# Two-layer encoder trunk, latent attention: the exponential one slot later, VectorE's masked maximum ahead of the low halves, and the rotary tables built under layer 0's down projection

## What is computed

```python
# rotary tables, needed by layer 1 alone
freqs = 500000 ** (-arange(half) / half)
cos, sin = cos(positions * freqs), sin(positions * freqs)

# layer 0
x = layer_norm(ALPHA * x + mixer_sb_fox(x, ...), ...)
x = layer_norm(ALPHA * x + (gelu(conv(x @ w_gate)) * (x @ w_up)) @ w_down, ...)

# layer 1: 16 query heads over one shared latent key of 256 numbers
logits = einsum('bqhd,bqkd->bqhk', q, k_sel) * scale      # k_sel: each query's best 256 keys
p = softmax(where(valid, logits, -inf))
ctx = einsum('bqhk,bqkc->bqhc', p, k_sel[..., 64:])
```

## Time and profile before

| | us |
|---|---|
| median of three runs | 3183.16 |
| the profiled execution | 3195.31 |
| its span in the profile | 3193.5 |
| TensorE busy / weight loads | 2943.2 / 1524.1 |
| VectorE busy | 1805.8 |
| GpSimd busy | 1442.3 |
| ScalarE busy | 1026.3 |
| mean granted TensorE clock | 0.975 |

### The profile page before, as it was taken

One profiled execution on the slowest core, in us unless ns is written; L12 is line 12 of the kernel. 1 busy time (PEld: TensorE's weight loads), 2 busy tenths in 40 slices (PEclk: granted clock), 3 DMA queues, 4 the chain that ended last, 5 costly groups with the idle time before them and its releaser, 6 DMA issues.

```text
span 3193.5 us, 45888 instructions
## 1 busy us (share of the span) xinstructions
PE 2943.2 (92%) x17190; PEld 1524.1 (48%) x17472; DVE 1805.8 (57%) x2540; ACT 1026.3 (32%) x1671; POOL 1442.3 (45%) x721
## 2 busy tenths in 40 slices
PE   5899997999999999959799999888889999999998
PEld 3556665444444444434344444555654444444443
DVE  7687556474444414154699999566655744444042
ACT  3556667112222200014653334445540221222000
POOL 3577221654344378644017776200006533443785
PEclk8999999999999999979899999999999999999999
DMA  4222321411111132211003222011103111111322
GB/s 145 65 57 63 74 57 27 165 54 53 53 52 46 53 106 93 86 60 53 13 6 126 105 105 90 32 51 39 39 26 120 53 53 53 52 46 53 112 99 99
DMA packets 96516, 218.24 MB, mean 68 GB/s; under 512 B 41328, under 2 KB 41456, under 8 KB 96416
## 3 DMA queue, kind: packets, MB, share of 16 engines
q1 hardware_dynamic: 54048, 195.74, 18.0%
q10 hardware_dynamic: 42368, 21.11, 2.8%
HBM read 176.92 MB, written 23.12 MB: 63 GB/s over the span
## 4 chain that ended last, share of the span: by engine, by line
PE 39%; DVE 8%; ACT 5%; issue 3%; POOL 1%; DVEq 0%; DMA 0%; ACTq 0%; POOLq 0%; SPq 0%
PE ps L301 24%; PE ps L312 8%; PE ps L1865 3%; DVE prob L1942 2%; DVE score L1588 1%; DVE pt_lo L1934 1%; PE ps L336 1%; ACT strip_w L1534 1%; ACT strip_w L1449 1%; ACT pt_hi L1913 1%; PE ps L1901 1%; PE ps L1681 1%; ACT prob L1923 1%; PE ps L1880 1%; POOL w_hi L271 0%
## 5 line engine op out<-in xcount | busy, mean ns | idle before, releaser
L271 POOL TENSOR_TENSOR w_hi<-w_stage,ones 128x1024 bf16<-128x1024 f32 x227 | 454.8, 2004 | 940.2 <-PE ps L301 540.3
L301 PE MATMUL ps<-xt_hi,w_hi 128*128 128x512 bf16 x1888 | 565.4, 380 | 33.9 <-ACT strip_f L1450 29.7
L301 PE MATMUL ps<-xt_lo,w_hi 128*128 128x512 bf16 x1889 | 566.0, 380 | 1.6
L301 PE MATMUL ps<-xt_hi,w_lo 128*128 128x512 bf16 x1880 | 563.6, 380 | 2.1
L274 POOL TENSOR_TENSOR w_lo<-w_stage,w_hi 128x1024 bf16<-128x1024 f32 x227 | 520.4, 2292 | 17.8
L301 PEld LDWEIGHTS ps<-xt_hi,w_hi 128*128 128x128 bf16 x1920 | 187.9, 98 | 259.6 <-issue 29.8
L301 PEld LDWEIGHTS ps<-xt_hi,w_lo 128*128 128x128 bf16 x1920 | 188.3, 98 | 227.7 <-issue 2.1
L301 PEld LDWEIGHTS ps<-xt_lo,w_hi 128*128 128x128 bf16 x1920 | 188.2, 98 | 227.4 <-issue 1.6
L1219 DVE SCALAR_TENSOR_TENSOR x_res<-x_res,ps 128x1024 f32<-128x1024 f32 x32 | 38.9, 1216 | 417.8 <-PE ps L312 417.8
L1347 DVE TENSOR_SCALAR conv_up<-gate_up,conv_w_up 128x1024 f32<-128x1024 f32 x44 | 78.4, 1782 | 283.2 <-ACT gate_up L1328 282.7
L312 PE MATMUL ps<-w_hi,hid_hi 128*128 128x512 bf16 x689 | 206.2, 379 | 5.6 <-DVE x_res L1219 4.0
(11 more groups left out here) (230 smaller groups left out, 5746.2 us busy)
## 6 DMA issues: line engine op xcount, KB each, us to landing
w_stage<-in_l_up SPq DMA_DIRECT2D x88, 512.0 KB, 3.3
w_stage<-in_l_down SPq DMA_DIRECT2D x88, 512.0 KB, 3.3
w_stage<-in_l_o SPq DMA_DIRECT2D x32, 512.0 KB, 3.9
w_stage<-in_l_q SPq DMA_DIRECT2D x32, 512.0 KB, 5.4
q_split<-q_out SPq DMA_DIRECT2D x32, 512.0 KB, 2.6
q_now<-q_split SPq DMA_DIRECT2D x16, 1024.0 KB, 4.9
w_stage<-in_l_qkv SPq DMA_DIRECT2D x24, 512.0 KB, 3.5
k_twice<-nk_hi ACTq DMA_DIRECT2D x32, 128.0 KB, 2.9
```

The costliest lines, as they stand in the source:

```text
L271: pool.tensor_tensor(w_hi[slot][:, 0:cols], w_stage[slot][:, 0:cols], ones[:, 0:1].to_broadcast([P, cols]), ALU.mult).then_inc(w_cast[slot ...
L301: mm = pe.matmul(ps[:, bank + h, :], w, a[:, k, h * HALF:(h + 1) * HALF], start=(first and k == k0 and m == 0), stop=(last and k == k1 - 1 ...
```

## The change

Three edits. (1) All rotary work (two loads, 22 VectorE instructions, 4 sines, 4 stores) moves from the opening and the heads stage to the down projection of layer 0, in front of its `accumulate(0)` on VectorE and its square roots on ScalarE; its buffers move onto `xt_hi`/`xt_lo`. In the opening ScalarE now copies the four query and key halves, issues the 12 query and key copies, and only then takes the two value halves. (2) In latent attention ScalarE takes the exponential of the slot before, not of its own slot. (3) VectorE takes maximum(s) and `neg_max`(s) before `pt_lo`(s-3).

```diff
@@ start_sync
-            sp.dma_start(pos_i[:, :], t_in["positions"]).then_inc(s_pos, 16)
-            sp.dma_start(rope_rows[:, :], t_in["rope_rows"]).then_inc(s_pos, 16)
@@ start_vector
-            rotary_angles(dve, 0)
@@
-        scratch = Room(room.at)
+        scratch = Room(xt_at)
+        rope_rows = scratch("rope_rows", [P, 4], F32)
@@ pair_scalar
-                    if prev is None and at == 0:
-                        act.wait_ge(s_tabst, 64)
@@ heads_scalar
-            rotary_sines(act, 0)
-            rotary_store(act, 0)
-            proj_evac_hi(act, 0, 0)
-            proj_evac_hi(act, 1, 0)
-            rotary_sines(act, 1)
             act.preload_act_table_set("sigmoid_and_others")
-            for e in range(2, 6):
+            for e in range(4):
                 proj_evac_hi(act, e, 0)
             for hh in range(2):
                 make_current_qk(act, hh, 0)
+            for e in range(4, 6):
+                proj_evac_hi(act, e, 0)
             for hh in range(2):
                 make_current_v(act, hh, 0)
-            rotary_store(act, 1)
@@ heads_vector
-            rotary_finish(dve, 0)
-            proj_evac_lo(dve, 0, 0)
-            proj_evac_lo(dve, 1, 0)
-            rotary_angles(dve, 1)
-            proj_evac_lo(dve, 2, 0)
-            proj_evac_lo(dve, 3, 0)
-            rotary_finish(dve, 1)
-            proj_evac_lo(dve, 4, 0)
-            proj_evac_lo(dve, 5, 0)
+            for e in range(6):
+                proj_evac_lo(dve, e, 0)
@@ new
+        def rotary_sync(sp):
+            sp.dma_start(pos_i[:, :], t_in["positions"]).then_inc(s_pos, 16)
+            sp.dma_start(rope_rows[:, :], t_in["rope_rows"]).then_inc(s_pos, 16)
+
+        def rotary_scalar(act):
+            for t in range(2):
+                rotary_sines(act, t)
+                rotary_store(act, t)
+            act.wait_ge(s_tabst, 64)
+
+        def rotary_vector(dve):
+            for t in range(2):
+                rotary_angles(dve, t)
+                rotary_finish(dve, t)
@@ back_and_norm, sync_program (dn0 alone)
                 if after:
                     sp.wait_ge(after["hidden_lo"], FT)
+                if rotary:
+                    rotary_sync(sp)
                 sp.dma_start(g_rows[:, :], names[0]).then_inc(s_gb, 16)
@@ latent_scalar
-                if kind:
-                    t, i, hh = slot, query_block(slot), slot // 8
+                p, t = steps_behind(act, pair, slot, kind, prev, 1)
+                if t is not None:
+                    i, hh = query_block(t), t // 8
                     n = span[i]
-                    act.wait_ge(t_nm, STEPS * pair + t + 1)
+                    act.wait_ge(t_nm, STEPS * p + t + 1)
@@ latent_vector: this block moves from before the maximum to after neg_max
                 p, t = steps_behind(dve, pair, slot, kind, prev, SUMS_LAG + 1)
                 if t is not None:
                     for n, j0, m in batch_list(t):
                         hi, lo, src = turned_views(t, n, j0, m)
                         dve.wait_ge(t_hi, BATCHES * p + n + 1)
                         dve.tensor_tensor(lo, src, hi, ALU.subtract).then_inc(t_lo, 1)
```

More of the change, by code:

```diff
@@ L200, in program @@
         w_lo = [wroom(f"w_lo{s}", [P, KT * P], BF16) for s in range(SLOTS)]
+        xt_at = wroom.at
         xt_hi = wroom("xt_hi", [P, KT, SEQ], BF16)
@@ L375, in program @@
         xt_f = room("xt_f", [P, KT, SEQ], F32)
-        rope_rows = room("rope_rows", [P, 4], F32)
         wf_f = room("wf_f", [P, KT, 8], F32)
@@ L969, in heads_sync @@
             load_first(sp, feed_o0)
-            sp.wait_ge(s_tabst, 64)
         def heads_gpsimd(pool):
@@ L1041, in back_and_norm @@
         def back_and_norm(tag, feed, tiles, act_hi, act_lo, names, free_at, bank_of, next_feed, early, load_x=None,
-                          final=None, after=None, started=None):
+                          final=None, after=None, started=None, rotary=False):
             room = Room(free_at)
@@ L1097, in sync_program @@
                     load_first(sp, next_feed)
+                if rotary:
+                    sp.wait_ge(s_tabst, 64)
                 if final is not None:
@@ L1194, in highs @@
                         act.activation(hi, src, ACT.Copy).then_inc(s_nh, 1)
+                if rotary:
+                    rotary_scalar(act)
                 for i in range(GROUP):
@@ L1246, in lows @@
                         dve.tensor_tensor(lo, src, hi, ALU.subtract).then_inc(s_nl, 1)
+                if rotary:
+                    rotary_vector(dve)
                 for i in range(GROUP):
@@ L1396, in program @@
             back_and_norm("dn0", feed_down0, FT, hid_hi, hid_lo, (t_in["l0_ln2_g"], t_in["l0_ln2_b"]),
-                          after_hid, (0, 4, 2, 6), feed_small, early_small(feed_small), after=up0_sems))
+                          after_hid, (0, 4, 2, 6), feed_small, early_small(feed_small), after=up0_sems, rotary=True))
         clear_sems()
@@ L1928, in latent_vector @@
             for slot in lat_slots(kind):
[L1929 to L1934, removed]
                 if kind:
@@ L1947, in latent_vector @@
                                       None, ALU.mult).then_inc(t_nm, 1)
+                p, t = steps_behind(dve, pair, slot, kind, prev, SUMS_LAG + 1)
+                if t is not None:
+                    for n, j0, m in batch_list(t):
+                        hi, lo, src = turned_views(t, n, j0, m)
+                        dve.wait_ge(t_hi, BATCHES * p + n + 1)
+                        dve.tensor_tensor(lo, src, hi, ALU.subtract).then_inc(t_lo, 1)
                 p, t = steps_behind(dve, pair, slot, kind, prev, SCALE_LAG)
```

## The result

Median of five runs 3198.9 us, against 3184.2 us for the kernel before on the same chip: ratio 1.0048, 95% interval 1.0034 to 1.0063, +14.7 us. The forecast was 3197 us, +13.5. The profiled executions don't show this difference: both spans are 3193.5 us. The changed kernel's is its fastest execution (3195.3 against a median of 3198.9), the one of before lies 11 us over its median of 3184.2.

The account below looks back on a forecast made before the run. TensorE, busy 2943 of 3193.5 us, was taken as the bound, so only its stands count. Opening -25.5, down projection 0, latent stage +37, clock +2 sum to +13.5 on 3183.2: 3197 us, range 3179 to 3226.

Parts of the forecast that it names:

- the main term: Latent stage: maximum ahead of `pt_lo` closes a new circle in which TensorE stands; +37 us, bounds 28 to 44.
- Opening: Opening: without rotary work ScalarE's first sigmoid comes earlier and TensorE stands less; -25.5 us, gain bounds 21 to 28.
- Down projection: Layer 0's down projection: added rotary work fits VectorE's 104.8 idle us, GpSimd stays ahead; 0 us, bounds 0 to +4.
- the exclusive lock: Down projection: skill's claim that VectorE and GpSimd fully block each other; by it the cost would be nearer +4.
- Latent stage at full clock: Latent halves grow from 24.15 to 26.74 and 26.29 us as TensorE waits for `pt_lo`; +37 us, bounds 28 to 44.
- Clock in the latent stage: Latent stage: TensorE's clock mostly stays up; +2 us, bounds 0 to 46 (16 halves x 2.9).
- rival C: Latent stage: clock falls in most halves, 12 x 2.9 = 35 us on top of 37, total 3230; chance 0.18.
- Rival A: Latent stage: freed ScalarE shortens the slots, at most 71 us; 3122 with half of it; chance 0.10.

Follow-up runs that it names:

- e1: Only the rotary move, latent stage as before, against the kernel before: 3167.2 us, ratio 0.9940.
- e5: Rotary move and exponential a slot later, VectorE's latent order kept, against the kernel before: 3093.3 us, ratio 0.9713.
- e6: As e5, but GpSimd's first weight piece waits for VectorE's last `xt_lo`: 3095.7 us against e5's 3093.3.
- e7: The kernel before, unchanged, profiled once more: span 3185.1 us against 3193.5 in its first profile.
- e2: Only the two latent edits (exponential a slot later, maximum ahead of low halves), no rotary move, against the kernel before: 3222.1 us, ratio 1.0111.
- e4: Only VectorE's maximum ahead of the low halves, exponential in its own slot, against the kernel before: 3220.8 us, ratio 1.0107.
- e9: As e2, but only the second batch of low halves of a slot goes behind the maximum, against the kernel before: 3147.0 us, ratio 0.9874.
- e3: Only the exponential a slot later, VectorE's low halves still ahead of the maximum, against the kernel before: 3116.3 us, ratio 0.978.

## Why the prediction was right, term by term

The forecast named the right mechanism for the main term and its place. That the total came within 1.2 us (+13.5 against +14.7) is luck: single terms were off by 6 to 9 us, with both signs.

**Opening, -25.5 predicted, -19 measured** (e1; first `stay` -20.2). What was mis-sized is one term: "Leaving the two loads out of SyncE's queue brings the first weight piece about 1.3 us earlier, but then GpSimd lies beside more of VectorE's `xt_lo`; between -1 and +1, I take 0". The piece was split from 13.45 on, not from 16.52, and lay beside all five `xt_lo`: 13.02 us instead of 7.65, projections from 27.18, ended at 58.57 instead of 53.8. That is +5 on the path of the value copies (+3 in e5). The term was named and mis-sized; its bounds would have had to be as wide as the slowing (3.04 against 1.21) over five instructions allows, 9 us. The gain, 20.2 at the first `stay`, lies outside the forecast's bounds of 21 to 28. The lower one stood for gate sums fully beside GpSimd, but 26.1 + 12.4 + 16 is 54.5, more than 9 us beyond the 45 of the same text. That the gate sums ended within the forecast 42 to 45 (43.4) is luck: their scan began at 31.75, some 5 us late, and they were hardly slowed. Full clock from 60 on (to 82) held; whether it gave back the 1.4 us no run separates, since e1's interval is 15 to 24 us.

**Down projection, 0 predicted, 0.0 measured** (104.79 against 104.78). GpSimd's first ten pieces took 4.5 to 5.9 us, 5.1 on average where the forecast had "near 5.9", and TensorE stood for none (busy 9.95 of every 10 us from 1104 to 1174). Against the exclusive lock (the Trainium skill, SBUF — State Buffer, Who interferes with whom) the forecast held that "both engines are slowed and neither stops". The rows don't show that: a row gives an instruction's start and length, not whether the engine stood within it.
```profile
1139.89 8.93 DVE L939 SCALAR_TENSOR_TENSOR angle<-turns,angle 128x1024 f32<-128x1024 f32 x3
1141.81 2.87 POOL L272 TENSOR_TENSOR w_hi<-w_stage,ones 128x1024 bf16<-128x1024 f32 x1
1144.75 2.99 POOL L275 TENSOR_TENSOR w_lo<-w_stage,w_hi 128x1024 bf16<-128x1024 f32 x1
```
In the 5.9 us of this piece VectorE does two of its three. Alone, the piece takes 4.0 us, and two such instructions 2.4 (the two `xt_lo` of e6), 6.4 together: close to taking turns, as by the lock. It would have each VectorE instruction cost GpSimd its whole 1.2 us; the piece grew by 1.9 for two. So the lock is neither refuted nor in full agreement here, and GpSimd kept ahead of TensorE, at 5.1 us a piece against 5.19.

**Latent stage at full clock, +37 predicted, about +28 measured.** The mechanism and its place were right, slot by slot: 4.19, 4.63, 3.91, 3.32 and 2.76 against 4.29, 4.72, 4.02, 3.41 and 2.85. Each is 0.1 too long in the forecast, mostly for one reason: `pt_lo` starts 0.99 us after the maximum (2030.92 to 2031.91), where the sum had 1.01 and a gap of 0.05, and the maximum starts 0.30 and not 0.31 after the last scores. Times five slots and 16 halves that is 8 us. The stage's tail, from the last slot's scores to the last values, was also 2.8 us shorter (6.7 against 9.5), and 1.4 of these are the clock: it fell in the tail of the first profile of before, and in e7, where it didn't, the tail is 8.1. The value lies at the lower bound of 28 to 44 (37 less and plus the 8 of the forecast would be 29 to 45).

**Clock in the latent stage, +2 predicted, +10.5 measured in the profile, 9 more than before.** The clock fell in eight halves of 16, each time at about the start of slot 4, and cost 0.8 to 1.6 us a time, not 2.9. Where it fell at the start, slot 4 took 5.22 us instead of 3.91, the 1.3 us that its own scores take longer at half clock; slot 5, which the forecast had slow too, kept its 3.32 to 3.35 in every half. So the frequency lies between the forecast ("a few halves") and rival C (12), and a fall cost about half or less of what both took. Rival C also misread: slot 3's 2.6 us of work in 4.7 is no share "between the two rows" but a larger one than either (2.62 and 2.40 of 5), and the clock fell all the same. The Trainium skill's TensorE: Matmul & The Clock Gate, HAM oscillation — how this bites in real kernels, which the forecast took to describe "just this", tells of a loop whose compute is shorter than its wait, cold again in every turn. Here the longest stand is 1.8 us in a half of 26, and the clock fell in 8 of 16 halves (6 in e2 and in e4), so the trace agrees only in that falls recur. Halves whose stand in slot 3 was shorter (1.16 to 1.29 us in e9, 1.0 before) or absent (e3, e5) never lost the clock; that the length of the stand decides was not tested by itself. The sum of both latent terms, 39, hit 37.1 (393.1 to 430.2 us from the first scores to the last values) because two errors, -9 and +7, cancelled.

**Rival A** asked that the freed ScalarE shorten the slots, "at most 8 x 8.9 = 71 us". That number was right for the other kernel: e3 gained 70. It failed here by the point that the prediction gave, slot 3 longer than 3.86 (4.63).

Still open: why the clock fell in eight halves and not in the others with the same instructions (e2 and e4 lost it in the same six halves, at nearly the same times), and how e6's loss splits.

## What to carry to other kernels

Before an engine's instructions are reordered, ask of each pair which other engine waits for it in the same slot, and whether the one moved ahead has its input already. Here an instruction that had to wait for TensorE was put ahead of one that was ready and for which TensorE waited. A long wait in the table (190.9 us) is worth time only if it lies on the ring that binds: its removal gave -70 us with one order of VectorE and nothing with the other. And when a change has two edits, run each alone: and then together: here they were -70 and +34.5 alone, and +36 together.

## What the runs showed of the hardware

- VectorE beside GpSimd: two `xt_lo` take 2.36 us alone (e6), five take 13.02 beside GpSimd's pieces, 2.6 each and not 1.2; GpSimd's `w_hi` and `w_lo` take 2.87 and 2.98 there against 1.89 and 2.12. Starting GpSimd earlier made the common path later (projections from 25.2 to 27.3 instead of 22.2 to 23.2).
- A stand in a loop can cost twice. After slot 3's 1.8 us the clock came down in half of the turns of the changed kernel, at 0.8 to 1.6 us a time. In e9, whose stand in slot 3 was 1.16 to 1.29 us, it stayed up in all.
- Two profiles of the same kernel differ by 8.4 us of span (0.26%), with 157 and 128 us at half clock and no other difference found, so a half per cent is to be read from stretches, or from medians.
